# Nine Python loops of a one-core two-block kernel become hardware loops

## The reference

```
h = _rmsnorm(x, norm_w); proj = h @ w_in           # 1024 x 10240, split into ten parts
q, f_fwd, f_bwd, i, g, u, v, g_b, m_a, m_b
y_a = hgrn2 branch: for 8 heads, forward and backward
      S_t = diag(f_t) S_{t-1} + k_t v_t^T ; o_t = S_t^T q_t
      rms norm over each head, times silu(g)
y_b = gelu(u) * (w_s @ layernorm(gelu(v)) + b_s) * silu(g_b)
merged = sigmoid(m_a) * (y_a @ w_proj_a) + sigmoid(m_b) * (y_b @ w_proj_b)
x = x + merged @ w_out ; final rms norm
```

## Time and profile before

| what | value |
|---|---|
| runs | 1757.66, 1762.83, 1764.28 us |
| the profiled execution | 1764.28 us, span 1762.5 us |
| PE busy | 1628.9 us, 92% |
| DVE, ACT, POOL busy | 759.8, 632.2, 481.0 us |
| head stage from its second iteration | 115 to 469 us |
| merge stage | 655 to 860 us |
| TensorE clock granted, mean | 0.962 of full speed |

### The profile page before, as it was taken

The page is one execution under the profiler, slowest core; times in us unless marked ns, Lnnn a source line. Parts: engine busy times, 40 slices in busy tenths (PEclk is TensorE's granted clock), DMA queues, the critical chain, the costliest instruction groups (busy, mean ns, idle before and its releaser), DMA issues.

```text
span 1762.5 us, 22431 instructions
## 1 busy us (share of the span) xinstructions
PE 1628.9 (92%) x9320; PEld 1296.3 (74%) x9320; DVE 759.8 (43%) x1302; ACT 632.2 (36%) x1014; POOL 481.0 (27%) x237
## 2 busy tenths in 40 slices
PE   5999999999899889999799998999998899999996
PEld 5888988889788667777688896555686765555565
DVE  2346266274574421110278612666515444444424
ACT  5322322312422322112442223666614424555632
POOL 3331222222222343433532232333432230010221
PEclk9999999999999989999899999999998999999998
DMA  5231212202323335344321121000021220000101
GB/s 179 97 120 48 91 54 72 96 25 73 88 80 96 104 112 191 120 133 130 104 75 49 49 80 48 19 19 19 1 63 48 59 60 10 10 19 25 49 25 48
DMA packets 129316, 122.76 MB, mean 70 GB/s; under 512 B 11348, under 2 KB 125152, under 8 KB 129216
## 3 DMA queue, kind: packets, MB, share of 16 engines
q1 hardware_dynamic: 129216, 121.33, 22.0%
HBM read 116.87 MB, written 2.10 MB: 67 GB/s over the span
## 4 chain that ended last, share of the span: by engine, by line
PE 73%; DVE 12%; DMA 4%; ACT 4%; POOL 3%; issue 3%; SPq 1%; DVEq 0%; POOLq 0%; ACTq 0%
PE ps L1944 8%; PE ps L1945 7%; PE ps L1946 7%; PE ps L1990 5%; PE ps L2424 3%; PE ps L2403 3%; PE ps L2413 3%; PE ps L2153 2%; PE ps L2152 2%; PE ps L2154 2%; PE ps L2255 2%; POOL w_lo L1089 2%; DMA raw<-in_w_in_dram 2%; DVE qf L1316 2%; DMA raw<-in_w_proj_b_dram 2%
## 5 line engine op out<-in xcount | busy, mean ns | idle before, releaser
L1089 POOL TENSOR_TENSOR w_lo<-raw,w_hi 128x2048 fp32r<-128x2048 f32 (+2 forms) x85 | 367.3, 4323 | 849.9 <-ACT w_hi L649 771.3
L1944 PE MATMUL ps<-h_hi,w_hi 128*128 128x512 f32 x632 | 257.9, 408 | 11.0 <-DVE g_lat L1788 4.5
L1946 PE MATMUL ps<-h_hi,w_lo 128*128 128x512 f32 x632 | 250.9, 397 | 0.0
L1945 PE MATMUL ps<-h_lo,w_hi 128*128 128x512 f32 x632 | 250.7, 397 | 0.0
L649 ACT ACTIVATE w_hi<-raw 128x2048 fp32r<-128x2048 f32 (+1 forms) x77 | 145.6, 1891 | 270.0 <-DMA raw<-in_w_in_dram 97.7
L1944 PEld LDWEIGHTS ps<-h_hi,w_hi 128*128 128x128 f32 x632 | 122.0, 193 | 42.2 <-issue 13.8
L1946 PEld LDWEIGHTS ps<-h_hi,w_lo 128*128 128x128 f32 x632 | 121.3, 192 | 26.8
L1945 PEld LDWEIGHTS ps<-h_lo,w_hi 128*128 128x128 f32 x632 | 122.1, 193 | 24.1
L1990 PE MATMUL ps<-qf,kf 128*128 128x64 f32 x448 | 88.7, 280 | 9.4 <-DVE tot_b L1319 6.2
L1037 ACT ACTIVATE pT_b<-ps 128x512 f32<-128x512 f32 x96 | 57.0, 595 | 94.1 <-PE ps L2413 92.9
L1990 PE MATMUL ps<-qb,kb 128*128 128x64 f32 x448 | 89.2, 282 | 0.0
(11 more groups left out here) (441 smaller groups left out, 3494.5 us busy)
## 6 DMA issues: line engine op xcount, KB each, us to landing
raw<-in_w_in_dram SPq DMA_DIRECT2D x32, 1024.0 KB
raw<-in_ada_w_dram SPq DMA_DIRECT2D x24, 1024.0 KB
raw<-in_a_w_in_dram SPq DMA_DIRECT2D x10, 1024.0 KB
raw<-in_w_in_dram SPq DMA_DIRECT2D x16, 512.0 KB
raw<-in_b_w_in_dram SPq DMA_DIRECT2D x5, 1024.0 KB
raw<-in_w_proj_a_dram SPq DMA_DIRECT2D x4, 1024.0 KB
raw<-in_w_proj_b_dram SPq DMA_DIRECT2D x4, 1024.0 KB
raw<-in_w_out_dram SPq DMA_DIRECT2D x4, 1024.0 KB
```

Source lines behind the costliest of these rows:

```text
L1089: nc.gpsimd.tensor_tensor(w_lo[:, ph.w(s), c], raw[:, s % 2, c], w_hi[:, ph.w(s), c].bitcast(F32), ALU.subtract).then_inc(s_lo, 1)
L1944: mm(ps[:, j, :], wh[:, k, c], xh[:, k, :], start=(k == 0), stop=False)
L1945: mm(ps[:, j, :], wh[:, k, c], xl[:, k, :], start=False, stop=False)
L1946: last = mm(ps[:, j, :], wl[:, k, c], xh[:, k, :], start=False, stop=(k == KT - 1))
```

## The change

Nine of the Python loops become hardware loops, one for each engine and stage but the merge stage of SP. The loop body then stands once in the engine's program; `it` is a register; semaphore values and addresses that depend on it are computed by register instructions, and a compare-and-branch at the end goes back to its head. The first iteration of `heads` stays written out, so the head loops run three times (two ways back) and the merge loops four times (three ways back).

```
 # @block.sync
-            for it in range(1, PAIRS):
+            with sp.Fori(1, PAIRS) as it:
                 heads_it(it)
 # @block.scalar
-            for it in range(1, PAIRS):
+            with act.Fori(1, PAIRS) as it:
                 head_tiles(it, False)
-            for it in range(0, merge.iters):
+            with act.Fori(0, merge.iters) as it:
                 merge_act(it)
 # @block.gpsimd
-            for it in range(1, PAIRS):
+            with pool.Fori(1, PAIRS) as it:
                 for s in heads.split:
                     lo(heads, it, s)
-            for it in range(0, merge.iters):
+            with pool.Fori(0, merge.iters) as it:
                 for s in merge.split[1:]:
                     lo(merge, it, s)
                 lo(merge, it + 1, 0)
 # @block.vector: the same two lines around head_tiles(it, False) and merge_dve(it)
 # @block.tensor: the same two lines around head_tiles(it, False) and the body of the merge stage
```

More of the change, by code:

```diff
@@ L1413, in _ @@
             head_tiles(0, True)
-            for it in range(1, PAIRS):
+            with dve.Fori(1, PAIRS) as it:
                 head_tiles(it, False)
@@ L1510, in merge_dve @@
                 dve.sem_inc(s_m, 1)
-            for it in range(0, merge.iters):
+            with dve.Fori(0, merge.iters) as it:
                 merge_dve(it)
@@ L2053, in _ @@
             head_tiles(0, True)
-            for it in range(1, PAIRS):
+            with pe.Fori(1, PAIRS) as it:
                 head_tiles(it, False)
@@ L2084, in _ @@
             pe.wait_ge(s_ybl, GCH)
-            for it in range(0, merge.iters):
+            with pe.Fori(0, merge.iters) as it:
                 for s, kind in enumerate(MERGE_STRIPS):
```

## The result

The changed kernel takes 1774.79 us (median of 7 runs, 1768.94 to 1781.12), the kernel before 1762.83 (7 runs, 1757.66 to 1766.01). The ratio is 1.0074, with a 95% interval from 1.0051 to 1.0096: 12 us slower, where I had forecast no change at 1763.5. The time lies at the upper edge of the range, 1775. The direction is that of rivals A, B and C, and slower had a chance of 0.24. The profiled execution took 1774.67 us with a span of 1772.9, 10.4 us longer than the span before.

The account below looks back on a forecast made before the run. The prediction took PE, busy 92% of the span, as the bound. Its terms, 0 + 0 + 0.3 + 0 + 0 + 0 + 0.8 - 0.5 = +0.6 us on 1764.28, gave 1764.9, a median of 1763.5; range 1757 to 1775.

Parts of the forecast that it names:

- Rival A: Slower, chance 0.12: PE's instruction supply is not ahead, so its five ways back cost 3.7 us each, 18.5 in all: 1782.
- Rival B: Slower, chance 0.14: VectorE's code fetch at the head stage's two ways back outlasts its cover, +5.2 us: 1769.
- Rival C: Slower, chance 0.10: register instructions cost PE 0.1 us at each of 104 places (tiles and steps), +10.4 us: 1774.
- point 4: PE's ways back, two in head stage, three in merge stage: supply runs ahead and hides the code fetch, cost 0.
- Point 1: VectorE's two ways back in the head stage: L1290 starts up to 2.3 us late, covered by GpSimd's operation, cost 0.
- Point 2: Register instructions holding VectorE's waits for PE at the head stage's levels: 0.2 us per level, covered, cost 0.
- Point 3: Head loop's exit, where PE waits for L1343: L1341 stands behind a waiting register instruction, +0.3 us, once.
- Points 5 and 6: PE's 180 register instructions run beside queued matmuls; ways back of ScalarE, GpSimd and SyncE fit in idle time: cost 0.
- Point 7: Merge stage, PE's four waits for `w_lo`: register instructions on ScalarE and PE add 0.2 us each, +0.8 us.
- Point 8: Tiles of head and merge stages: the matmul now holds the bank wait, recovering some "issue" time, -0.5 us.
- Rival D: Faster, chance 0.06: all 4.1 us of "issue" time comes back and PE holds its clock better, -8.9 us: 1754.

Follow-up runs that it names:

- e2: The kernel before with only TensorE's head loop made a hardware loop: 1776.99 us, ratio 1.0072.
- e6: The changed kernel with the head of TensorE's head loop placed at instruction 208 of its 256-instruction code block: 1764.21 us, ratio 1.0002.
- e5: The changed kernel with the head of TensorE's head loop placed at instruction 96 of its 256-instruction code block: 1760.71 us, ratio 0.9987.
- e7: The changed kernel with the head of TensorE's head loop at instruction 208 of its block and the branch-back hint armed: 1766.16 us, ratio 1.0005.
- e4: The changed kernel with the head of TensorE's head loop placed at the first instruction of a 16 KB code block: 1763.19 us, ratio 0.9985.
- e8: The kernel before, with VectorE waiting for ScalarE's kb copy ahead of L1290 at the two inner head ends: 1766.61 us, ratio 1.0028.
- e9: The kernel before, with VectorE waiting for the new pair's first product tile ahead of L1290 at the two inner head ends: 1768.44 us, ratio 1.0018.
- e10: A second timing of the kernel of e8: 1766.83 us, ratio 1.0006.

## Why the prediction was wrong

**The step that failed is point 4**: "if the supply is ahead by 2.0 us, or 9 matmuls of 0.23 us, a fetch costs nothing ... I take 0, because PE's tiles ran without gaps over 74 packets." The supply is ahead by 3.2 us, more than I asked for. What was wrong is the price of a fetch behind a branch and their number. The 2.0 us came from a transfer of data. A branch that missed took 3.4 to 5.5 us over e2, e6 and the changed kernel: at the first way back 2.1 us until the packet starts, 1.2 for the packet, and 1.5 until the branch ends. And the changed kernel needed two, one after the other; from where the supply stopped, its head stands two instructions ahead of a block's end, and e6, with 48 there, has no second gap. Tiles that ran without gaps over 74 packets showed only that fetching straight ahead is in time. They say nothing of a jump.

**Rival A** had the mechanism in part and not the place. Its condition, a supply that is not ahead, was not met: it was ahead, by less than the fetches last. It expected five ways back at 3.7 us each, 18.5 in all. Two cost anything, about 6 us each (idle and clock, less the `qb` wait), and the merge stage's three cost nothing: their branches took 0.21 to 0.23 us. That body has 484 instructions, 1.9 blocks, and stays. I had treated all five alike and did not ask how much code is kept, though the 64 bytes to an instruction and 16 KB to a packet would have turned a count of both bodies, weight loads included, into blocks. Rival C's 1774 is the figure nearest to the measured 1774.8, by chance: its mechanism is excluded below.

**The Trainium skill** ("Runtime: NRT & Kernel Launch", Instruction fetch mechanics), with its rule that a taken branch to a page outside the two that are held stalls, was right in kind for the one loop that lost and wrong on how much is held: e5 goes back over 7 blocks without a fetch. The same section also gives TensorE 128 KiB for its instructions, 2048 of them, and most other engines 512. I had weighed only the sentence on two pages. The figure of 2048, 8 blocks of 256, is what the runs bear out: e7 holds 8 touched blocks with the hint, while without it 7 stay (e4, e5) and 8 do not (e6), as if one were needed for fetching ahead. By the figure alone an estimate from the body of 1616 would have said that the loop fits at any position. Measured, the position decides. For VectorE's body of 146 instructions, whose branches took under 0.07 us, the trace agrees as well. The prediction's sentence that by the rule of two pages every way back of VectorE stalls did not follow: at the section's 256 instructions to a page, such a body need not leave them. The other page ("Advanced Engine Details and Errata", Engine Queue Depths) gives TensorE a queue of 64. Between the branch's dispatch and the end of L2028 the array still had some 10 matmuls of the tile and 8 transposes to run, 3.2 us. That is the lead to reckon with here; no run shows the depth of the queue itself.

**Point 1** (VectorE's way back, 0): right, for a reason I had not given. There was no fetch to hide: VectorE's branches took 0.06 and 0.07 us. L1290 started 0.7 us later behind the end of L2028 than before (3.9 us instead of 3.2), was shorter (3.34 us) and ended 1.1 us behind GpSimd. Only 0.2 of the 0.7 lie behind L1343, where at least 0.3 was to show it; the rest stands ahead of L1341. The cover that I had relied on is real too (e8 to e10). **Point 2** (register steps at the levels, 0): the third and sixth level unchanged, 2.6 us for `tot_b`; the waits for `tot_a` grew from 0.6 to 0.9 us in all, so +0.3. **Point 3** (exit, +0.3): 2.7 to 3.0 us. Right. **Points 5 and 6** (TensorE's 180 register instructions, the other engines' ways back, 0): right. e5 has all nine loops and their register instructions, and its interval ends at +1.1 us; rival C's 10.4 is excluded. **Point 7** (merge stage, +0.8) was too high. From 660 to 880 us in the changed kernel:

```profile
PEld ps L1944 <- issue: 8.5, 4, 2.9
...
PE ps L1944 <- POOL w_lo L1089: 6.6, 4, 2.5
...
PEld ps L1944 <- DVE merged L1503: 1.6, 4, 0.4
```

The wait for `w_lo` grew by 0.1 us in all. The first of these lines is no new loss; in the kernel before (650 to 870 us) it stands with the same numbers under the name of its releaser:

```profile
PEld ps L1944 <- POOL w_lo L1089: 8.5, 4, 2.9
```

**Point 8** (a gain of 0.5) was nothing. The last of the three lines is the 1.6 us that were put down to "issue" before, in the same four places, under a new name. In the head stage e4 has 1.2 + 1.2 us under two names where 2.5 stood before. The order in which waits are carried changed the label and not the time.

**Rival B** was excluded by the end of L1290. **Rival D** is not seen: the kernels without the stall lie between 0.9984 and 1.0006, and no interval is clear of 1. So no version beats the kernel before. What a loop saves in code, 12 of 68 packets, the DMA queues did not need.

## What to carry to other kernels

Before rolling a loop on the bounding engine, count the instructions of its body, weight loads and register instructions too, and set them against what the engine keeps. On TensorE here a body that touched 7 blocks of 256 instructions was free; the same body at a position where it touched 8 left PE idle for 3.5 to 10 us in two ways back, of which the 3.5 us of e6 cannot be told from zero in its time. Where it nearly fits, place the head so that the body touches one block less (its start does that best) or arm the hint. And look for a taken branch in the trace before you price one: packets that arrive in time going straight ahead, and transfers of data, say nothing of it.

## What the runs showed of the hardware that I had not expected

- TensorE kept a loop of 1616 instructions without fetching it again when it touched 7 blocks of 16 KB, and with the hint even when it touched 8. Touching 8 without the hint, it fetched every block again in each iteration (15 or 16 packets from 200 to 400 us, against 1 or none where it was kept).
- A branch back that hits takes 0.21 to 0.26 us on TensorE, under 0.07 us on the other engines. One that misses takes 3.4 to 5.5 us on TensorE. Between two misses of one loop the length differed by 1.6 us in e6 (3.87 and 5.49), in which the packet began 1.0 and 3.0 us behind the branch; why it began later is open.
- A stall of instruction supply has no name of its own in the waits. It stood as "issue" once and as a wait for `y_a` L1377 once, for the same event in the same loop. The packets of the code queue and the branch's own record tell it.
- The clock fell to 0.50 and 0.55 for 5 us behind idle stretches of 4.5 and 5.7 us, was 0.66 behind one of 2.5 us, and stayed at 1.00 behind one of 0.95 us.
